# A two-layer diffusion step on one core: the first norm and its products taken by halves of the inner dimension

## The reference

```
m = silu(c) @ w_mod[l] + b_mod[l]            # 6 vectors of 1024 per token group
sh1, sc1, g1, sh2, sc2, g2 = split(m, 6)
h = rmsnorm(x, norm1_g[l]) * (1 + sc1) + sh1
q, k, v, bg, cg, xc = split(h @ w_in[l], ...)
q, k = rmsnorm(q), rmsnorm(k)                # per head of 64; then rotary on latent tokens
o = diff_attention(q, k + cached k, v + cached v)
y = rmsnorm(bg * dwconv3(cg * xc))
x = x + g1 * (concat(o, y) @ w_out[l])
x = x + g2 * swiglu_with_dwconv3(rmsnorm(x) * (1 + sc2) + sh2)
```

## Time and profile before

| | us |
|---|---|
| median of 3 runs | 1639.06 (1638.63 to 1639.83) |
| profiled execution, its own time | 1643.47 |
| its span in the trace | 1641.6 |
| PE busy | 1580.3 (96%) |
| DVE busy | 1053.1 (64%) |
| ACT busy | 736.8 (45%) |
| first product of the first layer starts | 54.09 |

### The profile page before, as it was taken

How to read it: one execution, slowest core, us unless ns; L and a number is a source line. 1 busy time by engine, 2 the same in 40 slices (tenths; PEclk the granted TensorE clock), 3 DMA queues, 4 the chain that set the end, 5 groups by cost and what they waited for, 6 DMA issues and landing times. The chain is left out here.

```text
span 1641.6 us, 26517 instructions
## 1 busy us (share of the span) xinstructions
PE 1580.3 (96%) x10563; PEld 1469.4 (90%) x10563; DVE 1053.1 (64%) x1774; ACT 736.8 (45%) x1259; POOL 142.7 (9%) x172
## 2 busy tenths in 40 slices
PE   5999999998999999999989999999999999999998
PEld 4677888987999999999977788989899999999998
DVE  4763676735786674767768637576487758476573
ACT  2543444424663552635535444443366346164462
POOL 0000000000221201212000000000012021120210
PEclk7899999999999999999989999999999999999999
DMA  9455101173785866858533541114169477594862
GB/s 334 141 187 186 53 27 52 53 260 100 190 186 150 190 154 149 198 148 199 133 115 129 203 144 35 44 47 149 36 152 203 137 176 174 135 221 129 189 166 81
DMA packets 284172, 236.14 MB, mean 144 GB/s; under 512 B 10576, under 2 KB 254864, under 8 KB 284048
## 3 DMA queue, kind: packets, MB, share of 16 engines
q1 hardware_dynamic: 259520, 189.82, 37.0%
q0 software_dynamic: 23680, 44.05, 15.7%
q10 hardware_dynamic: 848, 0.56, 0.1%
HBM read 188.78 MB, written 3.67 MB: 117 GB/s over the span
## 5 line engine op out<-in xcount | busy, mean ns | idle before, releaser
L587 POOL DMA_DIRECT2D raw_all<-raw_all x160 | 137.9, 878 | 1133.2 <-DMA raw_all<-in_w_up_dram 999.8
L1441 ACT ACTIVATE w_hi<-raw_all 128x1024 fp32r<-128x1024 f32 x120 | 126.2, 1056 | 234.6 <-DMA raw_all<-raw_all 110.1
L1067 PE MATMUL ps<-gg,w_hi 128*128 128x322 f32 x704 | 219.1, 311 | 0.0
L1974 DVE TENSOR_TENSOR w_lo<-raw_all,w_hi 128x1024 fp32r<-128x1024 f32 x120 | 146.6, 1221 | 112.8 <-ACT w_hi L1441 112.3
L1069 PE MATMUL ps<-gg,w_lo 128*128 128x322 f32 x704 | 218.7, 311 | 0.0
L1068 PE MATMUL ps<-gg,w_hi 128*128 128x322 f32 x704 | 218.4, 310 | 0.0
L1012 PE MATMUL ps<-hc_lo,w_hi 128*128 128x322 f32 x640 | 199.6, 312 | 0.0
L1014 PE MATMUL ps<-hc_hi,w_lo 128*128 128x322 f32 x640 | 198.9, 311 | 0.0
L1010 PE MATMUL ps<-hc_hi,w_hi 128*128 128x322 f32 x640 | 198.7, 310 | 0.0
L1010 PE MATMUL ps<-ht_hi,w_hi 128*128 128x322 f32 x480 | 150.8, 314 | 6.8 <-ACT s L1459 4.7
L1870 DVE SCALAR_TENSOR_TENSOR x<-ps,modv,x 128x128 f32<-128x128 f32 (+2 forms) x240 | 90.3, 433 | 91.8 <-PE ps L1069 53.8
(11 more groups left out here) (207 smaller groups left out, 3515.3 us busy)
## 6 DMA issues: line engine op xcount, KB each, us to landing
raw_all<-in_w_up_dram SPq DMA_DIRECT2D x280, 256.0 KB, 3.8
raw_all<-raw_all POOLq DMA_DIRECT2D x160, 256.0 KB, 4.1
raw_all<-in_w_mod_dram SPq DMA_DIRECT2D x64, 512.0 KB, 4.4
raw_all<-in_w_in_dram SPq DMA_DIRECT2D x48, 512.0 KB, 4.7
raw_all<-in_w_down_dram SPq DMA_DIRECT2D x16, 768.0 KB, 4.4
raw_all<-in_w_down_dram SPq DMA_DIRECT2D x16, 640.0 KB, 4.2
raw_all<-in_w_out_dram SPq DMA_DIRECT2D x16, 512.0 KB, 4.4
pre_w<-in_w_mod_dram SPq DMA_DIRECT2D x8, 512.0 KB, 9.8
```

What stands on the lines that cost most here:

```text
L587: pool.dma_start(raw_f[:, BLK * dst:BLK * (dst + 1)], raw_f[:, BLK * src:BLK * (src + 1)], accum_op=ALU.add).then_inc(sum_full[which], 16)
L1067: mm(out, wh[:, k, :], gh, start=k == 0, stop=False)
L1441: A(whi_b[:, 2 * i:2 * (i + 1), :], src, ACT.Copy).then_inc(up_hi[i], 1)
L1974: V.tensor_tensor(wlo_b[:, pair, :], raw_b[:, pair, :] if i else first_pair(g), whi_b[:, pair, :].bitcast(F32), ALU.subtract).then_inc(up_ ...
```

## The change

The opening of the first layer is done by halves of the inner dimension. The modulation halves are made in the order 0, 2, 1, 3 (`PRE_ORDER`); with 0 and 2 there, the norm runs over k = 0 to 3 of all five tiles, then over k = 4 to 7 (`NORM_ORDER`), and PE takes the five units (0, t) and then the five (1, t). Halves 1 and 3 are summed and turned between the units (0, t). The statistics come from the rows of x as loaded: ACT squares each token tile with a row sum straight into `rms5`, and PE's `stat` of the first layer is gone. The DMAs are reordered accordingly; ACT issues its small DMAs ahead of the conditioning's Silu. The first four units of each layer's running modulation are loaded into buffers of their own, `mod_q`; for the second layer SP issues them ahead of the last quarter of the last down projection of the first. In both layers the transposes of the cached keys go behind all ten units, and ACT's `qk_copy(0)` goes behind the items of p = 0.

```diff
-PRE_BANKS = [7, 0, 1, 2]
+PRE_ORDER = [0, 2, 1, 3]
+PRE_BANKS = {0: 0, 2: 1, 1: 7, 3: 7}
+def norm_order(l):
+    if l == 0:
+        return [(t, 4 * half + k) for half in range(2) for t in range(NT) for k in range(4)]
+    return [(t, k) for t in range(NT) for k in range(KT)]
...
@@ SP
+            def first_mods(layer, us):
+                for u in us:
+                    sp.dma_start(mod_q[:, u, :].rearrange("p (t n) -> p t n", n=UC),
+                                 w_mod_v[:, layer * KT:(layer + 1) * KT, (u + 8) * UC:(u + 9) * UC]
+                                 ).then_inc(modq_full[u], 16)
...
                     for q in range(4):
+                        if q == 3 and c == len(CHUNKS) - 1 and l < LAST:
+                            sp.wait_ge(prod_done, 7 * S_LAYER * (l + 1))
+                            sp.wait_ge(taps_ready, 2 * N_GATE * (l + 1))
+                            first_mods(l + 1, range(4))
                         down_block(c, q)
...
@@ PE
+                def beside_first(b, t):
+                    if l == 0:
+                        if (b, t) in ((0, 0), (0, 2)):
+                            pre_sum(1 + t)
+                        elif (b, t) in ((0, 1), (0, 3)):
+                            mod_turn(None, t)
+                    if (b, t) == ((1, 0) if l else (1, 1)):
+                        first_pair_sum(0)
+                    elif (b, t) == ((0, 2) if l else (1, 2)):
+                        mod_turn(l, 0)
+                    elif (b, t) == ((0, 3) if l else (1, 3)):
+                        first_pair_sum(1)
...
+                if l == 0:
+                    first_units = [(b, t) for b in range(2) for t in range(NT)]
...
+                pe.wait_ge(kv_in, 16 * l + 16)
+                for s in range(4):
+                    ins = nc.tensor.transpose(ps[:, 5, s * P:(s + 1) * P], kc[:, s * P:(s + 1) * P], ident[:, :])
+                ins.then_inc(qkT_full, 1)
...
@@ ACT
+            for t in range(NT):
+                ins = A(xsq[:, t, :], xin[:, t, :], ACT.Square, accum_out=rms5[:, t:t + 1])
+            ins.then_inc(sum_ready, 1)
...
+            rows(None, 0)
             split_hi_of(0, 0)
+            act.wait_ge(lam_ready, 1)
+            A(lam_s[:, :], lam_s[:, :], ACT.Exp).then_inc(lam_exp, 1)
             rows(None, 2)
...
+                for i in range(NORM1):
+                    if l == 0 and i == NORM1 // 2:
+                        act.wait_ge(mod_used, 4)
+                        split_hi(1)
+                    norm_hi(i)
+                    if l == 0 and i in (11, 19):
+                        rows(None, 1 if i == 11 else 3)
...
-                qk_copy(0)
                 for p in range(3):
+                    if p == 1:
+                        qk_copy(0)
...
                     if p == 0:
-                        rows(l, 1)
+                        if l == 0:
+                            rows(l, 0)
+                        else:
+                            rows(l, 1)
...
                             item(p, t)
+                            if l == 0 and p == 0 and t == 3:
+                                rows(l, 1)
```

More of the change, by code:

```diff
@@ L84, in load_order @@
     split = [("split", n) for n in range(N_SPLIT)]
-    order = split[0:2] + mod[0:4] + split[2:4]
+    order = split[0:4]
     for h in range(2, 6):
@@ L353, in hybrid_step @@
             sem(s) for s in ("xr_ready", "hh2_ready", "h2_ready", "tsum_ready", "thi_ready", "t_ready"))
+        modq_full, v_in = [sem("modq_full%d" % u) for u in range(4)], sem("v_in")
         modx_full, modt_full = sem("modx_full"), sem("modt_full")
@@ L463, in _ @@
                     before, j = ORDER[l][r - 2]
-                    free_of_split(j) if before == "split" else free_of_mod(j + 1)
+                    if l or r not in (3, 4):
+                        free_of_split(j) if before == "split" else free_of_mod(j + 1)
                     kind, n = ORDER[l][r]
+                    if l == 0 and r == 3:
+                        sp.wait_ge(mod_used, 6)
+                        first_mods(0, (0, 1))
+                    elif l == 0 and r == 4:
+                        sp.wait_ge(mod_used, 8)
+                        first_mods(0, (2, 3))
                     if (kind, n) == ("split", O_U + 2):
@@ L724, in _ @@
             x_sample(range(0, KT))
+            spread(0, 0)
             pe.wait_ge(cT_ready, 1)
             pre_sum(0)
-            mod_turn(None, 0)
             pe.wait_ge(small_in, 16 * N_SMALL)
@@ L734, in _ @@
                 ins.then_inc(setup_full, 1)
[L735 to L744, removed]
+            mm(ps[:, 4, 0:256], ones[0:1, :], brow[0:1, 512:768], start=True, stop=True)
+            mm(ps[:, 7, :], ones[0:1, :], brow[0:1, 0:512], start=True, stop=True).then_inc(setup_full, 1)
+            mod_turn(None, 0)
+            pre_sum(2)
+            mod_turn(None, 2)
             for l in range(DEPTH):
@@ new lines, in first_pair_sum @@
+                def first_pair_sum(h):
+                    for u in range(2):
+                        mod_sum(l, h, u, "q", None)
+                def beside_first(b, t):
[10 more added lines that the diff above has]
+                        first_pair_sum(1)
@@ L1151, in _ @@
                 act.dma_start(vrow[0:3 * V_FT - P, l, 2, :], fr[P:3 * V_FT, :]).then_inc(ffn_in, 16)
[L1152 to L1160, removed]
+            act.wait_ge(c_in, 48)
+            A(crow[:, :], crow[:, :], ACT.Silu).then_inc(silu_c, 1)
+            act.sem_inc(sq_ready, KT)
+            act.wait_ge(x_in, 32)
+            for t in range(NT):
+                ins = A(xsq[:, t, :], xin[:, t, :], ACT.Square, accum_out=rms5[:, t:t + 1])
+            ins.then_inc(sum_ready, 1)
             def rms_of(l, which, scale):
@@ L1187, in rms, with norm_hi @@
                     rms_of(l, which, scale)
[L1189 to L1194, removed]
+                def norm_hi(i):
+                    t, k = NORM_ORDER[l][i]
+                    act.wait_ge(tmp_ready, NORMED * l + (i + 1))
+                    A(h_hi[:, k, TOK_TILES[t]:TOK_TILES[t] + P], tmp_t[:, i % KT, :], ACT.Identity,
+                      bias=modv[:, 0, k, TILE_SEQ[t]:TILE_SEQ[t] + 1]).then_inc(hh_ready, 1)
                 if l:
@@ L1198, in _ @@
                     split_hi(1)
[L1199 to L1203, removed]
-                            rows(l, 0)
+                for i in range(NORM1):
[5 more added lines that the diff above has]
+                        rows(None, 1 if i == 11 else 3)
+                    if l and i == 27:
+                        rows(l, 0)
                 def qk_copy(n):
@@ L1613, in _ @@
-            dve.wait_ge(lam_exp, 1)
-            V.tensor_tensor(neglam[:, :], lam_s[:, DEPTH:2 * DEPTH], lam_s[:, 0:DEPTH], ALU.subtract)
-            dve.drain()
-            for l in range(DEPTH):
-                V.tensor_scalar(neglam[:, l:l + 1], neglam[:, l:l + 1], -LAM_INIT[l], None, ALU.add)
-            for h in range(2):
-                mod_post(None, h)
+            for k in range(KT):
+                dve.wait_ge(xT_full, k + 3)
+                V.tensor_copy(x[:, k, C_SAMPLE:C_SAMPLE + DEC], ps[:, (2 + k) % 5, :]).then_inc(xT_read, 1)
```

225 lines of the change are left out of this document (120 added, 105 removed).

## The result

The changed kernel takes 1655.27 us (median of 4 runs, 1653.87 to 1657.69), the kernel before on the same chip 1638.85 (4 runs, 1636.19 to 1639.83): ratio 1.010, 95% interval 1.0086 to 1.0114. It is slower by about 16 us, as forecast (1655). The profiled execution of the changed kernel took 1654.33 with a span of 1652.5; the one before 1643.47 and 1641.6. So the two traces differ by 10.9 us and the medians by 16.4, and not everything that the forecast hit was hit for the reason it gave.

What follows compares the result with a forecast made beforehand. PE, busy 96% of the span, was taken as the bound, so new standstills count in full. First layer +6.7 and second +9.1 gave +15.8: 1643.47 to 1659.3, median about 1655, range 1646.5 to 1660.

Steps and rivals of the forecast that it cites:

- Part 1: First layer's opening: first product at 36.7 us, from 34.5 to 39.5, 17.4 earlier than before.
- Part 2: First layer, first product to E: PE stands 6.8 us at a turn; E at 87.3, 3.1 of 17.4 us left.
- E: Mark at the end of the first ten units, the first product of p = 1; 90.36 us in the kernel before.
- Part 3: First layer, E to Q: PE waits for the copy to kT; Q at E + 10.45, 7.2 us more, plus 2.6 clock.
- Q: Mark where PE transposes the normed queries; 93.60 us in the first layer of the kernel before.
- first rival: The copy to kT is not waited for, as ACT reaches it earlier: 1636, or 1634 with an early first product; chance 6%.
- None of it depends on what came before E: First layer: claim about the ACT and DVE chain from the end of (1,4) to the root of item (0,4), ending E + 9.84.
- Part 4: Second layer: the moved transposes and copy of the cached keys delay the query transposes, +6.5 us, with the clock +9.1.
- Part 5: The rest: early second-layer loads and the 640 KB behind them land near 826, with 6 us of room; priced at nothing.
- third rival: Loads for the second layer land near 837; PE stands some 4.5 us more and falls to half clock: 1662; chance 6%.
- clock loss of 2.6 per standstill: Half clock of PE behind each new standstill of several microseconds: 2.6 us taken, from 1.5 to 2.9, three times.
- 4.4 of the prediction: How far the earlier kernel's profiled execution stood above its runs' median; turned the forecast of 1659.3 into 1654.9.

Runs made afterwards that it cites:

- turn: Changed kernel with the first layer's first running half's row copy right behind the norm and its DVE bias ahead of the items: 1652.54 us, ratio 1.0068.
- b_kT_late: Kernel before with only the cached keys' transposes moved behind all ten units and the copy to kT behind the p = 0 items, both layers: 1656.71 us.
- kT1: Changed kernel with the cached keys' transposes and their copy back at their earlier places in the second layer alone: 1649.84 us, ratio 1.0064.
- b2: Kernel before, unchanged, run and traced a second time: 1638.57 us, ratio 0.9998.
- silu_first: Changed kernel with the condition's Silu ahead of ACT's small DMAs again: 1661.90 us, ratio 1.0134.
- kT01: As kT1, and in the first layer cached keys transposed behind the sums after (1,3), copied ahead of the weight split waiting for (1,4): 1643.01 us.
- kT01_turn: Changed kernel with the edits of kT01 and turn, and the second running half's row copy one item earlier: 1636.02 us, ratio 0.9973.

## Why the prediction was right

**Part 1, the first product.** The steps came close one by one: Silu 11.33 (9.7 + 1.28 = 11.0 predicted), transposes of x 12.02 (11.6), last copy 20.2 (20.1), root 18.15 (19.5), first product 35.11 (36.7). A square took 1.04, not 1.25, which was off the path anyway. The 1.6 us lie at the end of the chain, on DVE and then ACT:

```profile
30.80 0.42 DVE L1690 TENSOR_REDUCE lam_s<-lamp 128x4 f32<-128x256 f32 x1
...
31.37 0.58 ACT L1188 ACTIVATE mod_row<-ps 128x512 f32<-128x512 f32 x1
```

Up to DVE's last reduction the sum is right (31.4 predicted, 31.22 measured). The turn and the broadcasts took 0.6 less than the 3.5 put down, at full clock, but DVE was copying until 27.55 and could not use it. Then the prediction gives the exponential and the row copy 1.5 us, and they took 0.7 (to 31.95). And it counts the 3.8 us to the first product, which the earlier trace rows give from the start of the row copy (50.27), from the copy's end, so that the copy's 0.6 is in the sum twice.

The table loads end 0.01 to 0.02 us before the activation behind them (10.03 + 1.28 to 11.33; 837.46 + 1.28 to 838.75 before). The drain of about 1.38 us that the Trainium skill (ScalarE: Activation LUTs, What ACT_TABLE_LOAD costs) puts on top is not seen at either.

**Part 2, to E.** (1,0) starts 22.39 us after the first product (22.45 predicted), the turn 39.4 (39.8) after a wait of 6.35 (6.8), E comes after 49.1 (50.6). Most of what the prediction has too much here is the clock: behind this wait PE is at 0.50 to 77 and at 1.00 from 78, about 1.6 us of work lost, not 2.6. The cause is shown by turn: with that row copy ahead of the items the wait is gone.

**Part 3, E to Q.** 10.55 (10.45 predicted), with a wait of 5.65 (5.8). The first rival, that the copy is not waited for, is ruled out by these waits, and b_kT_late shows the same 10.55 on top of the old opening. "None of it depends on what came before E" holds for this order only: in turn, where E comes 7.8 us sooner behind the first product, DVE's items are the later ones and E to Q is 13.05. The clock behind it cost 1.7 (9.27 - 7.58), not 2.6.

**Part 4, the second layer.** The first product there is 3.0 later than before, Q 10.7, the third transposes 12.0 (916.80 against 904.76). That is +9.0 (+9.1 predicted), of which 7.7 is the wait (6.5 to 6.8 predicted) and 1.3 the clock (2.6): right by two errors of opposite sign. The wait is longer since the chain did not start with the end of the units here (E is 896.44). It started later, behind a root of ACT that waited 2.55 us for DVE's sum and starts at 897.06:

```profile
897.27 1.90 ACT L1233 ACTIVATE w_hi<-raw_all 128x2048 fp32r<-128x2048 f32 x1
```

E to Q is 11.45 here, and 10.55 in the second layer of b_kT_late, where ACT was free in time. kT1 takes this away: 5.4 in the medians, and Q at 901.67 instead of 907.89, although its first layer's Q came 1.3 later (96.06).

**Part 5.** "Price nothing" was right and its reason wrong. The last quarter was not there at 826. From ACT's timeline of the changed kernel:

```profile
833.13 1.27 ACT L1518 ACTIVATE w_hi<-raw_all 128x1280 fp32r<-128x1280 f32 x1 [6.70 <-DMA raw_all<-in_w_down_dram]
```

It landed 7 us later than worked out; 3.2 of these are the issue of the loads ahead of it, which began at 815.95 and not at 812.7. So the third rival's mechanism was half there. Of the 6 us of room nothing was left, but PE lost nothing: it lags 2.8 us behind the kernel before at the third transposes of the queries (104.01 against 101.18) and 2.95 at the start of the second layer's spread of sums (856.96 against 854.01). Where the rest of the 7 us comes from was not tried.

**The sum.** The prediction had +6.7 for the first layer and +9.1 for the second. The trace has +2.8 at the third transposes (104.01 against 101.18) and +9.0. The 3.9 between are the first product (1.6), the clock and tenths of part 2 (1.5) and the clock of part 3 (0.9). The term that was most mis-sized is thus the clock loss of 2.6 per standstill: it measured 1.3 to 1.7, which over three standstills is 3.2 too much. The prediction took it near the upper end of 1.5 to 2.9, from the 5.9 us of half clock in the earlier trace rows. That was the long case: b2 has less than 3 us behind the same wait, and the new standstills of the changed kernel have 2.8 to 3.6. It is not a case that never comes, though. From Q to the third transposes it takes 7.6 us at full clock, and behind the nine waits for `kT` in the traces of the changed kernel, b_kT_late, kT1, turn and silu_first it takes 8.9 to 9.4 eight times and 10.18 once, in the second layer of turn (903.64 to 913.82): a loss of 1.3 to 1.8, and once of 2.6.

From the traces alone the changed kernel would have come at 1638.9 + 10.9 = 1649.8. The runs gave 1655.3. Two things bear on that. The trace of the kernel before is slow in its opening: against b2 the third transposes come 6.5 us later (104.01 against 89.89 + 7.58), close to the 6.7 of the prediction, though most of that lead is gone again by 437 us. And a profiled execution is one draw. Those of the kernel before lie 4.4 and 4.8 above their medians and the changed kernel's 0.9 below; over all ten kernels they lie from 4.0 below (silu_first) to 5.9 above (kT01). So the 4.4 of the prediction is no fixed distance between a profiled execution and the median. The prediction erred by +4.9 in the trace (+15.8 against +10.9) and was corrected by an offset that belonged to one execution: it was right in direction and mechanism, and to 0.3 us by luck.

In the medians the way from 1655.3 to 1636.0 goes by 5.4 (kT1), 6.8 (kT01) and 7.0 (kT01_turn, with both row copies moved); by the ratios it is 5.9, 6.6 and 8.4. That they add up is no check, since each is a difference between neighbours. Three standstills of 6 to 8 us each cost 5 to 8 us, which no gain ahead of them could repay, since each hangs, in the changed kernel, on the work just before it.

Not settled: kT01 has no wait for `kT`, and both its Q stand where b2's stand (89.77 and 898.07 against 89.89 and 898.15), yet its median is 3.9 us over the kernel before. Its trace is 0.8 us behind b2's at 1106 us and 5.5 at the end, in code that the edit doesn't touch. But that execution is the slowest of its ten, 5.9 above their median, and no run tells whether it is the rule.

## What to carry to other kernels

An engine works its queue in order: when a cheap copy (0.58 us) is written behind a chain that waits for another engine, it costs whatever that chain waits, here 5.7 to 7.6 us per layer, and an earlier start doesn't help as long as the chain hangs on the work just before. So when an opening is made shorter, follow each product that the freed engine now needs first to its place in its producer's queue, and move that place too: the same opening lost 16 us with two copies at the wrong place and won about 4 us (2 to 7 by the interval) with three copies moved by a few instructions. And give the opening's statistics the first place on their engine: behind 7 us of DMA issues they cost 5 us at the first product, of which 1.8 came from the clock behind PE's longer wait. And before a trace is set against a median, see how far single executions of the same kernel lie apart: 8 us here, half of what was to be explained.

## What the runs showed of the hardware

- The same program's opening varied by 3.7 us between two executions; what differs in them is PE's granted clock (0.51 from 55 to 60 us in one, 1.00 from 55 to 56 in the other). The lead doesn't last: the table loads of ACT stood at 300.65 and 437.51 in the kernel before, and in b2 so:

```profile
296.91 1.28 ACT L1298 ACT_TABLE_LOAD   x1
...
437.31 1.28 ACT L1404 ACT_TABLE_LOAD   x1
```

  The stretch between took 136.9 us in the kernel before and 140.4 in b2. PE is busy for 127.9 us of it at a mean granted clock of 0.96 in the one, and for 131.0 at 0.94 in the other; DVE is busy for 77.9 in both. So here too the clock makes nearly all of the difference.
- Half clock behind a standstill held for different times: 2.8 to 3.6 us behind the three new waits of the changed kernel (5.65 to 7.61 us long), but 5.5 behind the same wait of 7.61 in the second layer of turn; 5.8 from the first product of the kernel before, 5.2 from that of the changed kernel and less than 3 from b2's, each behind a wait of 2.5.
- Keeping PE busy through a wait of 5.7 us with products that nobody reads kept the granted clock at 1.00 and saved 1.6 us behind it, where the late copy itself adds 7.3 us between E and Q (10.55 against 3.24).
